# Second mixer of a two-layer encoder: input blocks, gates, key and query preparation and the output chain in another order

## The reference

```
xc, gc, cq, ckv, kr = split(rmsnorm(x) @ w_in, [512, 512, 256, 128, 32])
u  = centred_conv(xc, 4 taps, bias)
r, i = sigmoid(u @ w_a + b_a), sigmoid(u @ w_x + b_x)       # for 2 directions, 8 blocks of 64
a  = exp(-8 r softplus(-lam));  b = sqrt(-expm1(2 log a)) * i * u
h  = scan(h = a h + b) forwards + scan backwards
oc = gelu(gc) * h
q  = rmsnorm(cq) @ wuq  (8 heads, 64 + 32, the 32 turned by rope)
k, v = rmsnorm(ckv) @ wukv (64 + 64);  k gets rope(kr), the same for all heads
od = softmax(q k^T / sqrt(96)) v
x  = x + concat(oc, od) @ w_out
```

## Time and profile before

| | us |
|---|---|
| median of 3 runs (1956.9 to 1958.61) | 1958.45 |
| the profiled execution | 1959.18 |
| its span | 1957.4 |
| PE busy | 1891.2 (97%) |
| DVE busy | 1348.5 (69%) |
| ACT busy | 906.3 (46%) |
| POOL busy | 243.1 (12%) |

### The profile page before, as it was taken

One profiled execution on the slowest core, in us unless ns is written; L12 is line 12 of the kernel. 1 busy time (PEld: TensorE's weight loads), 2 busy tenths in 40 slices (PEclk: granted clock), 3 DMA queues, 4 the chain that ended last, 5 costly groups with the idle time before them and its releaser, 6 DMA issues.

```text
span 1957.4 us, 31136 instructions
## 1 busy us (share of the span) xinstructions
PE 1891.2 (97%) x11220; PEld 1654.4 (85%) x11220; DVE 1348.5 (69%) x1894; ACT 906.3 (46%) x1521; POOL 243.1 (12%) x208
## 2 busy tenths in 40 slices
PE   6999999998989999999999999999999999999996
PEld 5899988776868889998888999888776788999885
DVE  6789843566779579884357888525785677888424
ACT  4455523427347535553243555324377543555322
POOL 2100000213213210000021000001156221000001
PEclk9999999999989999999999999999999999999998
DMA  4232332322210222323222233332321022333321
GB/s 154 68 121 92 108 128 86 101 87 54 72 60 27 81 87 95 120 86 129 98 79 103 87 107 107 111 104 86 113 72 34 23 77 84 108 107 107 113 102 43
DMA packets 36204, 177.14 MB, mean 91 GB/s; under 512 B 12688, under 2 KB 13072, under 8 KB 15520
## 3 DMA queue, kind: packets, MB, share of 16 engines
q1 hardware_dynamic: 33696, 172.55, 26.0%
q10 hardware_dynamic: 2240, 2.98, 0.4%
q0 software_dynamic: 192, 0.59, 0.1%
HBM read 174.01 MB, written 2.10 MB: 90 GB/s over the span
## 4 chain that ended last, share of the span: by engine, by line
PE 90%; DVE 5%; ACT 2%; POOL 1%; issue 1%; DMA 0%; POOLq 0%; ACTq 0%; DVEq 0%
PE ps L308 29%; PE ps L310 28%; PE ps L309 28%; PE ps L1419 1%; DVE wl L278 1%; DVE xgl L356 1%; ACT wh L274 1%; PE ps L1442 1%; PE ps L1049 1%; POOL xg L2225 1%; DVE small L1005 0%; PE ps L1180 0%; PE ps L997 0%; POOL acc L390 0%; PE ps L979 0%
## 5 line engine op out<-in xcount | busy, mean ns | idle before, releaser
L308 PE MATMUL ps<-xgh,wh 128*128 128x256 f32 (+1 forms) x1504 | 514.7, 342 | 24.2 <-DVE xgl L356 13.8
L310 PE MATMUL ps<-xgh,wl 128*128 128x256 f32 (+1 forms) x1504 | 505.8, 336 | 0.0
L309 PE MATMUL ps<-xgl,wh 128*128 128x256 f32 (+1 forms) x1504 | 505.7, 336 | 0.0
L278 DVE TENSOR_TENSOR wl<-raw,wh 128x2048 fp32r<-128x2048 f32 (+1 forms) x93 | 215.0, 2312 | 355.6 <-ACT wh L274 355.6
L308 PE MATMUL ps<-tmh,wh 128*128 128x256 f32 (+1 forms) x1344 | 414.3, 308 | 0.0
L309 PE MATMUL ps<-tml,wh 128*128 128x256 f32 (+1 forms) x1344 | 414.3, 308 | 0.0
L310 PE MATMUL ps<-tmh,wl 128*128 128x256 f32 (+1 forms) x1344 | 414.3, 308 | 0.0
L274 ACT ACTIVATE wh<-raw 128x2048 fp32r<-128x2048 f32 (+1 forms) x93 | 176.5, 1897 | 356.6 <-PE ps L310 355.4
L308 PEld LDWEIGHTS ps<-xgh,wh 128*128 128x128 f32 x1504 | 286.8, 191 | 60.0 <-issue 18.9
L309 PEld LDWEIGHTS ps<-xgl,wh 128*128 128x128 f32 x1504 | 286.9, 191 | 30.4 <-issue 2.9
L310 PEld LDWEIGHTS ps<-xgh,wl 128*128 128x128 f32 x1504 | 286.6, 191 | 29.7
(11 more groups left out here) (284 smaller groups left out, 2599.8 us busy)
## 6 DMA issues: line engine op xcount, KB each, us to landing
raw<-in_units SPq DMA_DIRECT2D x161, 1024.0 KB, 4.9
x<-in_xT ACTq DMA_DIRECT2D x4, 512.0 KB, 7.7
outT<-x SPq DMA_DIRECT2D x8, 256.0 KB, 2.1
relb<-in_rpb SPq DMA_DIRECT2D x64, 24.0 KB, 2.2
cosA<-in_rope_a ACTq DMA_DIRECT2D x1, 256.0 KB, 2.6
sinA<-in_rope_a ACTq DMA_DIRECT2D x1, 256.0 KB, 2.9
cosD<-in_rope_d POOLq DMA_DIRECT2D x1, 256.0 KB, 3.2
sinD<-in_rope_d POOLq DMA_DIRECT2D x1, 256.0 KB, 3.0
```

Of the source, the lines that this page charges most:

```text
L278: nc.vector.tensor_tensor(wl[:, c % 2, 0:n], raw[:, c % 2, 0:n], wh[:, c % 2, 0:n].bitcast(F32), ALU.subtract).then_inc(w_lo, 1)
L308: nc.tensor.matmul(dst, lh, rh, start=first, stop=False, skip_group_check=onto)
L309: nc.tensor.matmul(dst, lh, rl, start=False, stop=False, skip_group_check=onto)
L310: return nc.tensor.matmul(dst, ll, rh, start=False, stop=last, skip_group_check=onto)
```

## The change

- Input blocks: cq, ckv and kr come first (blocks 0 to 3), then xc (4 to 7), then gc (8 to 11). The gates' unit is one later; gc's blocks 8 and 9 share a unit ahead of the gates' in use, block 9 is between gates 1 and 2, blocks 10 and 11 come after the gates.
- The two sums of squares stand after block 3, in PSUM banks 5 and 6.
- The convolution's first tap is on ACT (`conv_first`), the other three on DVE. The copies of cq and ckv into their high parts go from DVE to ACT, between the sigmoids of gates 1 and 2.
- The lower bound of th (eight DVE instructions, L2090) is gone; the root has 2**-115 as its bias instead.
- The eight roots (ACT) and the eight products into `bt` (POOL) move behind the heads. `bt` is now `iu` itself; `qnh`, `qnl` lie over the first half of `xgh`, `xgl`; `knh`, `knl` over `u32`, `xcp`; `qrh`, `krh` and their low parts no longer lie over anything of the gates.
- The preparation is interleaved with the first heads' scores: key 0, values, rotary query 0, query 0, turn, key 1 and so on; the scores of heads' steps 0 and 1 run before queries 2 and 3.
- The third unit of w_out is split on ACT ahead of the high parts of the channel groups, on DVE after channel group 0.
- The scratch for descriptors is 1024 instead of 4096 bytes.

The core of the diff:

```diff
-        INB = ([(BO + i // 2, i % 2, P) for i in range(4)] + [(BO + 2, 0, P), (BO + 2, 1, P), (BO + 3, 0, P),
-               (BO + 3, 1, P)] + [(BO + 5 + i // 2, i % 2, P) for i in range(4)])
+        INB = [(BO + i // 2, i % 2, P) for i in range(10)] + [(BO + 6, i, P) for i in range(2)]
...
+            odd_block_pe(pe, 2)
+            odd_block_pe(pe, 3)
+            pe.wait_ge(csq_sum, 1)
+            nc.tensor.matmul(ps[:, 5, :], ones[:, :], sqt[:, 1, :], start=True, stop=True).then_inc(cs_done, 1)
+            pe.wait_ge(csq_done, 3)
+            nc.tensor.matmul(ps[:, 6, :], ones[:, :], acc[:, :], start=True, stop=True).then_inc(cs_done, 1)
+            for i in range(4, 9):
                 odd_block_pe(pe, i)
...
             for g in range(8):
                 c, d = g // 2, g % 2
+                if g == 2:
+                    odd_block_pe(pe, 9)
...
+            key(kn_bank(0), 0)
             for t in range(TT):
...
             pe.wait_ge(w_lo, U_UQ + 1)
+            pe.wait_ge(in_read, 11)
+            query_pe(2, 512)
+            pe.wait_ge(in_read, 12)
+            query_pe(qn_bank(0), 0)
+            pe.wait_ge(r_sin_done, 1)
+            pe.wait_ge(qr32_done, 1)
+            turn(4, qr32[:, 0, :])
+            pe.wait_ge(kn_lo, 1)
+            key(kn_bank(1), 1)
+            query_pe(2, 640)
+            pe.wait_ge(qn_lo, 1)
+            query_pe(qn_bank(1), 128)
+            mla_scores_pe(pe, 0, 0)
+            pe.wait_ge(qr32_done, 2)
+            pe.wait_ge(r_sin_done, 2)
+            turn(4, qr32[:, 1, :])
+            mla_scores_pe(pe, 0, 1)
             pe.wait_ge(vd_lo, 3)
+            key(kn_bank(2), 2)
             pe.wait_ge(vd_lo, 4)
+            key(kn_bank(3), 3)
+            mla_scores_pe(pe, 1, 0)
+            mla_scores_pe(pe, 1, 1)
+            query_pe(qn_bank(2), 256, True)
+            pe.wait_ge(qn_lo, 2)
+            query_pe(qn_bank(3), 384)
...
+            sig(0)
+            sig(1)
+            u_hi_act(3)
+            for k in range(3):
+                act.wait_ge(cqn_done, k + 1)
+                nc.scalar.activation(cqh[:, k, :], cq[:, k, :], ACT.Copy).then_inc(cq_hi, 1)
+            sig(2)
+            sig(3)
             split_hi(act, U_GATE + 1)
+            for g in range(4, 8):
+                sig(g)
+            split_hi(act, U_UKV, n=1024)
...
             mla_act(act)
+            for g in range(8):
+                act.wait_ge(vv_done, g + 1)
+                nc.scalar.activation(th[:, g, :], th[:, g, :], ACT.Sqrt,
+                                     bias=col(C_TINY)).then_inc(mult_done, 1)
             for c in range(4):
                 act.wait_ge(in_read, 9 + c)
                 nc.scalar.activation(gc[:, c, :], gc[:, c, :], ACT.Gelu_apprx_tanh).then_inc(gelu_done, 1)
+            split_hi(act, U_WO + 2)
...
+            cs_rec(0)
+            evac(4)
+            split_lo(dve, BO + 3)
+            conv_dve(dve, 0)
+            evac(5)
+            u_lo_dve(0)
+            cs_rec(1)
+            split_lo(dve, BO + 4)
+            conv_dve(dve, 1)
+            evac(6)
+            u_lo_dve(1)
+            evac(7)
+            split_lo(dve, U_GATE)
...
+            od_lo_dve(dve, 3)
             oc_dve(0)
-            od_lo_dve(dve, 3)
-            oc_dve(1)
-            oc_lo_dve(0)
             dve.wait_ge(w_lo, U_WO + 2)
             split_lo(dve, U_WO + 2)
+            oc_lo_dve(0)
+            oc_dve(1)
             oc_lo_dve(1)
...
             mla_pool(pool)
+            for g in range(8):
+                first = SEQ - 1 if g % 2 else 0
+                pool.wait_ge(mult_done, g + 1)
+                nc.gpsimd.memset(th[:, g, first:first + 1], 1.0).then_inc(one_done, 1)
+                pool.wait_ge(one_done, g + 1)
+                nc.gpsimd.tensor_tensor(bt(g), iu[:, g, :], th[:, g, :], ALU.mult).then_inc(bt_done, 1)
             finish_pool(pool, 5)
```

More of the change, by code:

```diff
@@ L1422, in mla_scores_pe @@
                         mm.then_inc(SM["scores"] if half else half_done, 1)
-                    if i == 0 and half == 0 and s == 0 and t == 0:
+                    if i == 2 and half == 0 and s == 0 and t == 0:
                         mm.then_inc(w_half, 2)
         def mla_pe(pe):
-            for i in range(19):
-                if 1 <= i < 16:
+            for i in range(2, 19):
+                if i < 16:
                     mla_scores_pe(pe, i, 0)
@@ L1847, in odd_pe @@
             norm_pe(pe, 4, 4)
[L1848 removed]
+            odd_block_pe(pe, 2)
[5 more added lines that the diff above has]
+            for i in range(4, 9):
                 odd_block_pe(pe, i)
[L1851 to L1852 removed]
+            pe.wait_ge(cstd_done, 2)
             pe.wait_ge(std_done, 5)
[L1854 to L1856 removed]
             pe.wait_ge(w_lo, U_GATE + 1)
@@ L1873, in odd_pe @@
                         mm.then_inc(w_half, 2)
-            for i in range(8, N_IN):
+            for i in range(10, N_IN):
                 odd_block_pe(pe, i)
@@ L1886, in turn, with key, query_pe @@
                 nc.tensor.matmul(ps[:, bank, :], permD[:, :], src, start=True, stop=True).then_inc(prep_done, 1)
-            def query(bank, o, free=False):
+            def key(bank, a):
+                three(ps[:, bank, :], wh[:, sk, a * P:(a + 1) * P], wl[:, sk, a * P:(a + 1) * P],
+                      cqh[:, 2, :], cql[:, 2, :], True, True).then_inc(prep_done, 1)
+            def query_pe(bank, o, free=False):
                 for k in range(2):
@@ L1971, in odd_act @@
-            split_hi(act, U_GATE + 2)
+            act.wait_ge(pad_done, 2)
+            for k in range(2):
+                act.wait_ge(in_read, k + 1)
+                nc.scalar.activation(sqt[:, k, :], cq[:, k, :], ACT.Square).then_inc(csq_done, 1)
+            act.wait_ge(in_read, 3)
+            nc.scalar.activation(acc[:, :], cq[:, 2, :], ACT.Square).then_inc(csq_done, 1)
+            cs_sqrt(0)
+            cs_sqrt(1)
+            split_hi(act, BO + 3)
+            conv_first(0)
+            u_hi_act(0)
@@ L2000, in odd_act @@
                 nc.scalar.activation(krh[:, v, :], r_sin(0), ACT.Copy, scale=col(C_KR + v)).then_inc(r_hi, 1)
-            for b in range(2):
-                act.wait_ge(prep_done, 10 + b)
-                nc.scalar.activation(qr32[:, b, :], ps[:, 5 + b, :], ACT.Copy, scale=MS).then_inc(qr32_done, 1)
-            qn_hi_act(act, 0)
+            vd_hi_act(act, 2)
+            vd_hi_act(act, 3)
+            kn_hi_act(act, 1)
+            qr32_act(act, 1)
+            qr_hi_act(act, 0)
             qn_hi_act(act, 1)
-            qr_hi_act(act, 0)
+            kn_hi_act(act, 2)
+            kn_hi_act(act, 3)
+            mla_exp_act(act, 0)
             qn_hi_act(act, 2)
@@ L2078, in odd_dve @@
                                                ALU.mult, ALU.mult).then_inc(cqn_done, 1)
-            for k in range(3):
-                dve.wait_ge(cqn_done, k + 1)
-                nc.vector.tensor_copy(cqh[:, k, :], cq[:, k, :]).then_inc(cq_hi, 1)
+            evac(9)
+            split_lo(dve, U_GATE + 1)
             for k in range(3):
@@ L2437 @@
     small[:, 0] = EPS
+    small[:, 8] = 2.0 ** -115
     small[:, 2] = np.arange(P) % 64 < 32
```

277 lines of the change are left out of this document (123 added, 154 removed).

## The result

The changed kernel takes 1962.63 us (median of 20 runs, 1959.6 to 1964.81) where the kernel before takes 1958.39 beside it: ratio 1.0023, 95% interval 1.0016 to 1.0030. Run once more, beside experiment 8, it gave 1962.5 and 1.0026 (1.0018 to 1.0035). It is slower, by some 4.2 us.

The account below looks back on a forecast made before the run. TensorE bounds the kernel, busy 97% of 1957.4 us; changes pay only where it idles or runs at its lower clock. Front -4.0 plus output chain +8.6 gave +4.6 us, median 1963.0; range 1953.5 to 1967.5.

Parts of the forecast that it names:

- Part 1: Second mixer, latents first, to the gates: fp32 sums without wait, last blocks end 1445.9 instead of 1448.3, 2.4 us gained.
- Part 2: Preparation and first heads: fifth step starts at 1481.25 against 1486.87, 5.6 us gained; 4.0 taken, bounds 9 and 1.
- The heads: The twelve steps after the fifth step's start keep their work and are PE's, at 4.42 a step.
- Part 3: Output chain: late roots and POOL products make PE wait 6.3 us at the fourth unit, slow restart 2.3; loss 8.6.
- The sum: Whole kernel: -4.0 + 8.6 = +4.6 us, forecast on the median 1963.0 us.
- Rival (a): Output chain hardly late, scans not held by POOL: fourth unit 2.6 late, no slow restart, 1955.5 us; chance 0.2.
- Rival (b): Front gains more, 9 to 10 us, the 3.2 wait for evicted blocks vanishing: 1956 to 1959 us; chance 0.15.
- (c): More slow stretches: front 1, tail 10, so +9 us, 1967.5 us; chance 0.1.
- (d): Ahead of the gates, the sums of squares still wait for the POOL sum; small; chance 0.03.
- The two signs of being wrong: PE's wait for a weight split in the output product under 3 us, or the fifth step starting before 1478.

Follow-up runs that it names:

- experiment 8: Changed kernel with channel group 1's 24 matmuls issued once more ahead of the fourth output unit (counted twice in the output): 1959.88 us, ratio 1.0006 to the kernel before.
- experiment 6: Changed kernel with POOL's products inside the heads' last eight steps and the roots behind the heads, applied to the product (other output): 1959.0 us, ratio 1.0012.
- experiment 4: Changed kernel with the last two gates' blocks evicted on DVE right behind the query weights' split: 1964.09 us, ratio 1.0027.
- experiment 7: Changed kernel with the three copies of cq and ckv into their high parts back from ACT on DVE: 1962.18 us, ratio 1.0027.
- experiment 5: Changed kernel without the eight roots (other output), POOL's eight products one a step in the heads' last eight steps: 1954.57 us, ratio 0.9987.
- experiment 1: Changed kernel without the eight roots (other output), POOL's eight products run ahead of the heads: 1961.91 us, ratio 1.0019.

## Why the prediction was right

1963.0 was forecast, 1962.63 measured: slower, through the mechanism named. By its steps:

- *Part 1.* The fp32 sums lost their wait and their slow restart, as said. The gates' waits for sigmoids came where I put them, at 0.62 and 1.11 where I had 1.5 and 1.9; the last block ends 70.2 after the norm (1444.01 and one slot, less 1374.02) where I had 71.4. No slow stretch came between.
- *Part 2.* The wait for the evicted blocks was 2.40 (I had 3.2), with a slow stretch behind it; the one before the first scores 2.04 (1.3), the later ones together 1.93 (0.9: two for POOL, one for a DVE low half). The terms miss by 0.7 to 1.2 each, part 1's among them, some one way and some the other, and cancel, which is luck: the fifth step starts 106.73 after the norm, and 1481.25 - 1374.50 = 106.75 was my plan. So the worked sum of 5.6 was right, and the 4.0 that I took for it, for slow stretches that did not come, was not. The granted clock is 1.00 from 1460 to 1545.
- *The heads* keep their length: 59.02 us from fifth step to output product before and after. Right.
- *Part 3.* Less the front's gain, the plan and the trace are: first scan 1549.1 and 1549.27 (1548.79 and 0.48, the difference of the two norms, which the next two hold as well); group 3's end 1575.7 and 1576.0; fourth unit's low half 1580.6 and 1580.8; the wait 6.3 and 6.41; the slow restart 2.3 and 1.7 (experiment 8). Loss 8.6 and 8.40. The taking of turns, from rows with products only, held for scans: 4.47 us for two that take 2.34 alone. Here the Trainium skill's rule (SBUF — State Buffer, "Who interferes with whom") bore out: a DVE instruction with two SBUF inputs contends with a POOL instruction that reads SBUF, and here a scan is held like the rest. "Fully blocks", which I took for the loser, is said there of DVE's two-port modes; of the pair of ports in general the page says that it is an exclusive lock. The rows here agree with a lock held for an instruction's length. POOL's last two products:

```profile
1560.50 1.58 POOL L2286 TENSOR_TENSOR iu<-iu,th 128x512 f32<-128x512 f32 x1
...
1562.19 2.05 POOL L2286 TENSOR_TENSOR iu<-iu,th 128x512 f32<-128x512 f32 x1
```

  The second scan of the pair ends at 1565.32, 1.08 us behind the second product, nearly the whole length of a scan alone (1.17), as if it had begun when the product was done. The first two scans, at 1548.79 and 1551.13, took 1.23 each, and there it was POOL's products that grew, to 2.2.
- *The sum.* -4.0 + 8.6 = +4.6 agrees with the medians (+4.2) by luck. In the traces the terms are -5.57 and +8.40, with 0.37 gained behind: +2.5, of which the span shows 2.0, since the mixer starts 0.5 sooner. The trace after stands 1.5 us below its median and the one before 0.8 above, which makes up the rest. The changed kernel's four executions under 1960.1 us show a mean granted clock of 0.990, its five of 1964 us and more 0.987 to 0.989, so longer slow stretches are likely in the latter. Where they lie no trace shows; that is open.
- *Rival (a)*, tail hardly late: refuted, the scans are held. Its kernel without POOL beside the scans exists (experiment 6) and still waits 3.2, for roots. How much of the 3.3 us that it brings is holding, and how much the products' own time between root and scan, no run separates. *Rival (b)*: a wait of 2.40 with a slow restart of 1.7 was there beside the gain of 5.57, but its removal didn't pay: experiment 4 takes the wait away and others take it over. Its range was also added up wrong: a front of 9 to 10 and a tail of 6 to 8.6 give 1954.5 to 1958, not 1956 to 1959. *(c)* and *(d)* did not occur. The two signs of being wrong didn't either: the wait was 6.41, and the fifth step started at 1480.75.

What I did not see was the middle way. ACT sits idle for keys 2 and 3 in the front, 4.66 us in the changed kernel, as its timeline shows; that holds four roots and a table load (2.56 + 1.28). I had looked at "roots before the heads" and "roots behind" alone.

```profile
1465.84 1.29 ACT L2071 ACTIVATE knh<-ps 128x512 fp32r<-128x512 f32 x2 [4.66 <-PE ps L306]
```

## What to carry to other kernels

When work is moved off a bound stretch to where engines seem idle, follow it to its last consumer and count what runs beside it; here 5.6 us were gained at the fifth step and 8.4 lost some 90 us later, 3.3 of it because POOL's products stand between roots and scans and beside them. An idle gap of PE names the operation that came last, not the engine's queue behind it: pulling that operation forward on a full engine moved the gap (2.40 to 0.47, and a new one of 3.1). Moving work between engines also shifts who meets whom: in experiments 4 and 7 one POOL product beside DVE cost 1.0 us or more. And moves need not be whole: half of the roots (2.56 and a table load of 1.28) fitted into a gap of 4.66 us; all eight (5.0 and 1.28) would not, by their durations, though that was not run.

## What the runs showed of the hardware

- Two `TENSOR_TENSOR_SCAN`s take 2.33 us alone and 4.47 beside POOL's products; a POOL product takes 1.29 alone, 2.2 beside a scan and 3.40 beside a DVE weight split. POOL's timeline of the changed kernel:

```profile
1548.87 2.22 POOL L2286 TENSOR_TENSOR iu<-iu,th 128x512 f32<-128x512 f32 x1
...
1556.97 3.40 POOL L2286 TENSOR_TENSOR iu<-iu,th 128x512 f32<-128x512 f32 x1
```

- Adding 5.4 us of matmuls to a wait of 6.4 made the kernel 2.9 us faster, of which 1.7, by the output product's length, are the restart at the 1.2 GHz level that PE was spared.
- After the wait of 3.2 us in experiment 6 the restart was slow as well (3.4 us at half the clock), after the waits of 0.7 and 1.0 in experiments 5 and 8 it was not (clock 1.00).
- POOL products placed beside DVE's busy stretch cost the front 6.7 us, slow stretches included (experiment 1), those placed in the heads' steps cost nothing that shows (experiment 5, fifth step and start of the output product within 0.06 us of the changed kernel).
